# The rows of the recurrent block's gates three at a time on VectorE, with ScalarE's next weight roundings between them

## The reference

```python
proj = h @ w_in
xa, za, xb, gb, gc, zb = jnp.split(proj, [...], axis=-1)
ua = centred_dwconv(xa, conv_w, RG_CONV_LEFT) + conv_b
ya = rg_lru(ua, gate_w[0], ..., False) + rg_lru(ua, gate_w[1], ..., True)
ya = ya * jax.nn.silu(za.astype(jnp.float32))
yb = gb * centred_dwconv(gc * xb, sc_w, SC_CONV_LEFT)
yb = yb * jax.nn.silu(zb)
y = jnp.concatenate([ya, yb.astype(jnp.float32)], axis=-1) @ w_out
```

## Time and profile before

| | us |
|---|---|
| median of 3 runs | 1901.49 (1900.53 to 1905.0) |
| the profiled execution | 1901.67 |
| its span, first to last instruction | 1899.6 |
| TensorE busy | 1821.3 (96%) |
| VectorE, ScalarE, GpSimd busy | 801.8, 749.0, 778.5 |
| mean granted TensorE clock | 0.985 |

### The profile page before, as it was taken

How to read it: one execution, slowest core, us unless ns; L and a number is a source line. 1 busy time by engine, 2 the same in 40 slices (tenths; PEclk the granted TensorE clock), 3 DMA queues, 4 the chain that set the end, 5 groups by cost and what they waited for, 6 DMA issues and landing times.

```text
span 1899.6 us, 20384 instructions
## 1 busy us (share of the span) xinstructions
PE 1821.3 (96%) x8018; PEld 1439.9 (76%) x8018; DVE 801.8 (42%) x1392; ACT 749.0 (39%) x1176; POOL 778.5 (41%) x360
## 2 busy tenths in 40 slices
PE   7999999999999999899999999999899899999987
PEld 6887778888888786488888888777677687767665
DVE  3793542210221299632200211687677322245563
ACT  4523444322332365453322423454244332454432
POOL 3343224444444379544444444434334343333211
PEclk9999999999999999999999999999999899999999
DMA  5232113323333332023333233322331222422101
GB/s 184 82 97 78 45 49 96 100 91 98 100 99 90 93 96 67 0 86 94 98 99 100 89 100 99 112 81 75 100 96 61 80 98 69 115 67 67 56 23 45
DMA packets 100094, 160.31 MB, mean 84 GB/s; under 512 B 7296, under 2 KB 30208, under 8 KB 100000
## 3 DMA queue, kind: packets, MB, share of 16 engines
q1 hardware_dynamic: 100000, 159.02, 27.3%
HBM read 156.90 MB, written 2.10 MB: 84 GB/s over the span
## 4 chain that ended last, share of the span: by engine, by line
PE 83%; DVE 9%; ACT 3%; issue 3%; POOL 1%; DMA 1%; SPq 0%; POOLq 0%; ACTq 0%; DVEq 0%
PE bank L585 24%; PE bank L587 24%; PE bank L586 24%; PE bank L834 2%; PE bank L877 2%; POOL w_lo L2324 1%; DVE gla_state L2240 1%; DVE rg_t L2038 1%; PE bank L665 1%; PE bank L1031 1%; DVE rg_t L2027 1%; PE bank L1014 1%; ACT prob L1252 1%; PE bank L768 1%; DMA gate_w<-in_rg_gate_w 1%
## 5 line engine op out<-in xcount | busy, mean ns | idle before, releaser
L2324 POOL TENSOR_TENSOR w_lo<-w_raw,w_hi 128x1024 fp32r<-128x1024 f32 (+1 forms) x286 | 691.2, 2423 | 1071.6 <-ACT w_hi L1129 1071.6
L585 PE MATMUL bank<-x_hi,w_hi 128*128 128x512 f32 (+1 forms) x1264 | 508.4, 402 | 18.4 <-POOL w_lo L2324 16.3
L1129 ACT ACTIVATE w_hi<-w_raw 128x1024 fp32r<-128x1024 f32 (+1 forms) x286 | 299.6, 1054 | 557.4 <-PE bank L587 552.2
L586 PE MATMUL bank<-x_lo,w_hi 128*128 128x512 f32 (+1 forms) x1264 | 495.6, 392 | 0.0
L587 PE MATMUL bank<-x_hi,w_lo 128*128 128x512 f32 (+1 forms) x1264 | 495.3, 392 | 0.0
L585 PEld LDWEIGHTS bank<-x_hi,w_hi 128*128 128x128 f32 (+1 forms) x1264 | 238.7, 189 | 78.5 <-POOL w_lo L2324 17.2
L586 PEld LDWEIGHTS bank<-x_lo,w_hi 128*128 128x128 f32 (+1 forms) x1264 | 238.6, 189 | 54.9 <-issue 5.4
L587 PEld LDWEIGHTS bank<-x_hi,w_lo 128*128 128x128 f32 (+1 forms) x1264 | 238.4, 189 | 52.0
L585 PE MATMUL bank<-w_hi,f_hi 128*128 128x512 f32 x512 | 200.0, 391 | 0.0
L587 PE MATMUL bank<-w_hi,f_lo 128*128 128x512 f32 x512 | 199.3, 389 | 0.0
L586 PE MATMUL bank<-w_lo,f_hi 128*128 128x512 f32 x512 | 199.2, 389 | 0.0
(11 more groups left out here) (275 smaller groups left out, 2080.4 us busy)
## 6 DMA issues: line engine op xcount, KB each, us to landing
w_raw<-in_mlp_w SPq DMA_DIRECT2D x128, 512.0 KB, 3.7
w_raw<-in_even_w_in SPq DMA_DIRECT2D x48, 512.0 KB, 3.8
w_raw<-in_dsa_w_in SPq DMA_DIRECT2D x28, 512.0 KB, 3.5
w_raw<-in_odd_w_in SPq DMA_DIRECT2D x24, 512.0 KB, 3.6
w_raw<-in_conv_w_pw SPq DMA_DIRECT2D x32, 256.0 KB, 3.0
w_raw<-in_even_w_out SPq DMA_DIRECT2D x16, 512.0 KB, 4.2
w_raw<-in_dsa_w_out SPq DMA_DIRECT2D x8, 512.0 KB, 3.7
w_raw<-in_conv_w_pw SPq DMA_DIRECT2D x8, 512.0 KB, 3.8
```

The costliest lines, as they stand in the source:

```text
L585: e.matmul(o, sh, mh, start=first, stop=False)
L586: e.matmul(o, sh, ml, start=False, stop=False)
L1129: e.activation(hi, src, ACT.Copy).then_inc(*w_hi.up(u))
L2324: e.tensor_tensor(lo, src, hi.bitcast(F32), ALU.subtract).then_inc(*w_lo.up(u))
```

## The change

On VectorE the loop over zb's four rows becomes a loop of six steps: step i scales row i, multiplies row i-1 and subtracts for row i-2. za's loop becomes one of five steps: scale row i, multiply row i-1. On ScalarE zb's loop has five steps: Silu of row i, rounding of row i-1. Ahead of zb's and of za's rows stands a `split_to` for the next product's fourth unit, and before rows 1 and 3 one for one more unit each. On SyncE the gate weights of direction 1 are issued three unit loads earlier. What is computed doesn't change.

```diff
@@ scalar_program
                 for k in stream(f"zb{g}"):
                     if k in (1, 2):
                         roots(g, 1, (2 * k - 2, 2 * k - 1))
-                for j in range(4):
-                    w.wait_ge(*zb_in.at(g, j))
-                    e.activation(silu[j % 2][:, :], silu[j % 2][:, :], ACT.Silu).then_inc(*zb_silu.up(g, j))
-                    w.wait_ge(*yb_mul.at(g, j))
-                    e.activation(YBH[:, 4 * g + j, :], sc[:, j, :], ACT.Copy).then_inc(*yb_hi.up(g, j))
+                split_to(UNITS[f"zb{g}"][-1] + 1 + RING)
+                for i in range(4 + 1):
+                    if i in (1, 3):
+
+                        split_to(UNITS[f"zb{g}"][-1] + 1 + RING + (i + 1) // 2)
+                    if i < 4:
+                        w.wait_ge(*zb_in.at(g, i))
+                        e.activation(silu[i % 2][:, :], silu[i % 2][:, :], ACT.Silu).then_inc(*zb_silu.up(g, i))
+                    if i >= 1:
+                        w.wait_ge(*yb_mul.at(g, i - 1))
+                        e.activation(YBH[:, 4 * g + i - 1, :], sc[:, i - 1, :], ACT.Copy).then_inc(*yb_hi.up(g, i - 1))
             for g in range(2):
                 for k in stream(f"za{g}"):
                     pass
+                split_to(UNITS[f"za{g}"][-1] + 1 + RING)
                 for j in range(4):
+                    if j in (1, 3):
+                        split_to(UNITS[f"za{g}"][-1] + 1 + RING + (j + 1) // 2)
                     w.wait_ge(*za_in.at(g, j))
@@ vector_program
-                for j, b in enumerate(BANKS[f"zb{g}"]):
-                    if j >= 2 or g:
-                        w.wait_ge(*(yb_mul.at(g, j - 2) if j >= 2 else yb_mul.at(0, j + 2)))
-                    by_row(2, silu[j % 2][:, :], b, done(f"zb{g}"), zb_in, g, j)
-                    w.wait_ge(*zb_silu.at(g, j))
-                    w.wait_ge(*gb_row.at(g, j))
-                    e.tensor_tensor(sc[:, j, :], sc[:, j, :], silu[j % 2][:, :], ALU.mult).then_inc(*yb_mul.up(g, j))
-                    w.wait_ge(*yb_hi.at(g, j))
-                    e.tensor_tensor(YBL[:, 4 * g + j, :], sc[:, j, :], YBH[:, 4 * g + j, :].bitcast(F32),
-                                    ALU.subtract).then_inc(*yb_lo.up(g, j))
+                for i in range(4 + 2):
+                    if i < 4:
+                        if i >= 2 or g:
+                            w.wait_ge(*(yb_mul.at(g, i - 2) if i >= 2 else yb_mul.at(0, i + 2)))
+                        by_row(2, silu[i % 2][:, :], BANKS[f"zb{g}"][i], done(f"zb{g}"), zb_in, g, i)
+                    if 0 <= i - 1 < 4:
+                        j = i - 1
+                        w.wait_ge(*zb_silu.at(g, j))
+                        w.wait_ge(*gb_row.at(g, j))
+                        e.tensor_tensor(sc[:, j, :], sc[:, j, :], silu[j % 2][:, :],
+                                        ALU.mult).then_inc(*yb_mul.up(g, j))
+                    if i >= 2:
+                        j = i - 2
+                        w.wait_ge(*yb_hi.at(g, j))
+                        e.tensor_tensor(YBL[:, 4 * g + j, :], sc[:, j, :], YBH[:, 4 * g + j, :].bitcast(F32),
+                                        ALU.subtract).then_inc(*yb_lo.up(g, j))
...
+                    if i >= 1:
+                        j = i - 1
+                        w.wait_ge(*za_silu.at(g, j))
+                        w.wait_ge(*scanned.at(g, 1, j))
+                        e.tensor_tensor(ya[:, 4 * g + j, :], ya[:, 4 * g + j, :], silu[j % 2][:, :],
+                                        ALU.mult).then_inc(*ya_mul.up(g, j))
@@ sync_program
-            load_to(UNITS["gb0"][0] + AHEAD + RAW)
+            load_to(UNITS["xb0"][1] + AHEAD + RAW)
             w.wait_ge(*gate_mm.at(0, 0, 1, 3))
             load_gates(0, 1)
             up_to("zb0")
             w.wait_ge(*gate_mm.at(0, 1, 1, 3))
             load_gates(1, 0)
-            load_to(UNITS["gb1"][0] + AHEAD + RAW)
+            load_to(UNITS["xb1"][1] + AHEAD + RAW)
             w.wait_ge(*gate_mm.at(1, 0, 1, 3))
             load_gates(1, 1)
```

More of the change, by code:

```diff
@@ L2114, in vector_program @@
-            for g in range(2):
[L2115 to L2124, removed]
+                for i in range(4 + 2):
[14 more added lines that the diff above has]
+                                        ALU.subtract).then_inc(*yb_lo.up(g, j))
@@ new lines, in vector_program @@
+            for g in range(2):
+                for i in range(4 + 1):
+                    if i < 4:
+                        if i >= 2 or g:
+                            w.wait_ge(*(ya_mul.at(g, i - 2) if i >= 2 else ya_mul.at(0, i + 2)))
+                        else:
+                            w.wait_ge(*yb_mul.at(1, i + 2))
+                        by_row(2, silu[i % 2][:, :], BANKS[f"za{g}"][i], done(f"za{g}"), za_in, g, i)
+                    if i >= 1:
[4 more added lines that the diff above has]
+                                        ALU.mult).then_inc(*ya_mul.up(g, j))
```

## The result

The changed kernel takes 1885.11 us (median of 4 runs, 1881.46 to 1885.77) against 1901.01 (1897.61 to 1905.0) for the kernel before: a ratio of 0.9912, 95% interval [0.9888, 0.9935]. It is 15.9 us faster; 17.8 were forecast. The profiled execution took 1885.77 us, its span is 1883.7, the mean granted clock 0.988.

The account below looks back on a forecast made before the run. The prediction took TensorE as the bound, busy 1821.3 of 1899.6 us. It summed -10.1 - 10.4 - 0.3 + 1.2 + 1.8 = -17.8 us from 1901.67 to 1883.9, and forecast a median of 1883.7, range 1877.5 to 1891.

Parts of the forecast that it names:

- part 1: Rounding xa1[3] and za0[3] ahead of the rows removes TensorE's 8.2 us stalls and their slow clock: -10.1 and -10.4 us.
- slow clock: TensorE at 1.2 instead of 2.4 GHz after a stall; priced at 2.35 us per group behind the sigmoid waits.
- part 2: Rows interleaved: zb's end 0.9 us later, costing +1.2 us (0.8 to 2.9) at the convolution; a small wait goes, -0.3.
- part 3: Gate weights three loads earlier: DMA waits of 2.8 us go, sigmoid waits of 3.7 come; together +1.8 us (-2.9 to +3.1).
- the gain needs only the first split: At zb's and za's rows: the gain comes from the one rounding ahead, even if the rows don't pass faster.
- their interleaving pays only for the splits: At zb's rows: the new order only offsets GpSimd's splits among them; rows end 0.9 us later, not earlier.
- (B): VectorE becomes the bound at the turn of the groups, two more held operations and slow clock: 1890 us, chance 0.15.
- (D): Only one of the two long stalls at xa1 and za0 goes: 1894 us, chance 0.05.
- (E): Slower: ScalarE's waits in za1's rows hold x_hi, so x_lo comes after eout_b0: 1907 us or more, chance 0.03.
- (C): The clock doesn't fall in the new waits and VectorE's delay is hidden: 1878 us, chance 0.11.

Follow-up runs that it names:

- the best two kernels: Changed kernel with third and fourth gate-product pairs of direction 1 one row block later, 1874.91 us; with all four later and SyncE's old order, 1873.32 us.
- e2_first_only: Kernel before with only the rounding of one unit ahead of the rows of zb and za, rows in old order: 1895.21 us, ratio 0.9972.
- e3_rows_only: Kernel before with only the new order of the rows, no rounding moved, SyncE as before: 1884.24 us, ratio 0.9913.
- e6_pairs_later: Changed kernel with third and fourth pair of direction 1's gate products one row block later, on TensorE and ScalarE: 1874.91 us, ratio 0.9862.
- e5_splits_old_rows: Kernel before with all roundings moved as in the change, rows in their old order, SyncE as before: 1886.97 us, ratio 0.9927.

## Why the prediction was right, and where it was not

- **The long stalls** (part 1): forecast -10.1 and -10.4 us, measured -9.88 and -10.28 at VectorE's rows. Stall and slow clock both went, as the stretch table says. By TensorE's own stretches xa1 gives 10.1 and za0 10.8.
- **VectorE at the turn of the groups** (part 2): forecast +1.2 us between 0.8 and 2.9, measured +1.19. The wait for rg_u is 1.5 us. The steps up to the rows' end were right too: two multiplications held by 1.9 and 2.2 us for 2.1, the scans pushed by 2.0, the rows took 12.0 us for 12.4 and end 0.4 us later than before's 1352.0 moved by gb0's 1.70, for 0.9. That the sum meets 1.2 so closely is luck: the lateness is 0.3 us (xa1 ends at 1353.80, the convolution starts at 1354.09) and not 0.8, and the convolution takes 20.0 us and not 18.9, where the prediction chose 0.4 between nothing and one split of 2.1. Counted on TensorE, from xa1's end, the turn costs 1.4. One reading was wrong: the prediction says that how the rows' multiplications behave beside a split isn't shown. No row of its groups does, but the trace before has one of the same kind and shape, rg_i times rg_t beside GpSimd's three splits. It takes 0.68 us alone, and there:

```profile
1326.40 2.88 DVE L2034 TENSOR_TENSOR rg_i<-rg_i,rg_t 128x512 f32<-128x512 f32 x1
```

- **The gate weights** (part 3): forecast +1.55 and +0.25, measured +0.96 and -0.28. The new waits of 3.75 us stand where the prediction put them. The mis-sized term is the slow clock, 2.35 us taken as the mean of two rows: the pair after the stall came after 6.21 and 6.27 us in place of 4.48, so 1.7 and 1.8. With these the prediction's own terms give +0.9 and -0.3. Expected gain of the edit: none; the runs say the same, and the best two kernels show that the place of the products was the lever.
- **The sentence that failed**: "the gain needs only the first split", and with it "their interleaving pays only for the splits". With only that rounding moved, the stall comes back one unit later and 5.3 us are gained (e2_first_only); the interleaving alone gains 16.2 (e3_rows_only). The sum came out since all parts were there together. The step that failed was: I worked out when gc1[0] is ready only with the roundings between the rows in place, and never for the case that I then spoke of. And I compared the length of the rows with the splits among them to their length before, 0.9 us more, which hides that the same order without splits shortens them by 5.8 (13.6 to 7.8 us).
- **The end**: the block gave 18.4 us (17.8 forecast), the execution 15.9 and so did the medians. Of the rest, 0.7 lies ahead of the block. From za1 to the end the changed kernel took 1.8 us longer than before, with the same work. So the 1.9 us between forecast and measurement are of the size by which executions of the same work differ. The last stretch, from the same wait for x_lo to the end (before, then after):

```profile
1864.53:1899.60 35.07, 27.47 (x120) 22.39 (x120) 11.89 (x24) 8.92 (x23) 6.06 (x3) 0.92 0.15 60
```

```profile
1846.99:1883.70 36.71, 29.11 (x120) 23.53 (x120) 11.90 (x24) 8.90 (x23) 6.03 (x3) 0.88 0.14 58
```

Both have the same 120 matmuls. After, they run at a mean clock of 0.88 and not 0.92, and the stretch takes 1.6 us more. Over the ten traces, the part behind za1 lasts from 375.2 to 377.9 us with the same work. That the clock makes the difference is read in these rows; what sets where it falls was not tried. So a difference of up to some 2.7 us between the spans of two of these traces need not be about their edits.
- **The rivals**: (B), (D) and (E) did not come; no wait for x_lo stands before eout_a0. Of (C) nothing came either: the clock fell in both new waits. The rule of the Trainium skill, page "ScalarE: Activation LUTs", section "Table sets: the hidden batching unit", to batch the functions of one table set, changes nothing here, as forecast. The trace after agrees with what that page says of copy: the roundings between Silus have no load.

## What to carry to other kernels

When an in-order engine feeds the bound one and also takes part in a back-and-forth with another engine, both cures work on the same stall: put the feeding step ahead of the exchange, or shorten the exchange by taking its items two or three deep. Their gains don't add, and each must be worked out alone, with what is late next, before one says which of them makes the gain. A wait removed ahead of another wait on the same engine is worth only the distance between them: find the last one first (here the bank that a sigmoid frees) and move the work that asks, not the data that comes.

## What the runs showed of the hardware

- TensorE's clock and short stalls. After stalls of 2.38 and 2.34 us the clock stayed at 2.4 GHz (e3_rows_only, both places), and so it did after the waits of 1.0 us in e6_pairs_later and of 1.5 us in the changed kernel. After 2.79 and 2.81 us (before), 3.75 twice (changed) and 4.77 (e2_first_only) it ran at 1.2 GHz for a while; where the next pair of gate products tells the cost, it was 1.6 to 3.0 us. But the length alone doesn't decide it. In e5_splits_old_rows it fell after 2.61 us (the line with 0.57 above), and in e2_first_only it stayed up after 2.97, in the 8 us from the restart on:

```profile
1421.54 1.96 PE L877 MATMUL bank<-rg_u,gate_w 128*128 128x512 f32 x4 [2.97 <-DMA gate_w<-in_rg_gate_w]
```

```profile
1421.54:1429.54 8.00, 8.00 (x28) 5.30 (x29) 7.38 (x11) 0.30 (x1) 0.00 (x0) 1.00 0.14 50
```

What else decides it was not tried. I had expected the slow clock behind 3.0 us and put it into e3's expectation; it stayed away, and a stall that shrinks by 5.8 us gained 7.5. Another execution could lose some of that again.
- GpSimd's subtraction beside VectorE: a multiplication of two SBUF tensors took 2.54 and 2.88 us beside it, 0.69 alone. The convolution's first rows, which read a bank, took no longer beside it: from 1354.69 on three of them took 1.88 us together, while GpSimd's splits ran from 1354.52 to 1359.5. The moved splits cost VectorE 23.7 us of busy time in all, and the kernel 1.2 of it at gc1. At both places, xa1 and za0, VectorE goes from zb's rows to the next without idle, but only behind xa1's rows does TensorE soon want VectorE's result; before gc1's, gb1's and za1's rows VectorE still idles 8.4, 4.1 and 6.8 us.
